# Two-layer transformer stack on one core: loads kept out of a recurrence, attention output and values by token block, gates spread without diagonals

## The reference

```
x = x + rwkv7(rms_norm(x))            # projections k, r, v, g and a small "lora"; recurrence in 4 chunks of 64 tokens
kb, vb = shared_kv(x)                 # k1, v1
x = x + moba(rms_norm(x), kb, vb)     # q1, gate g1; with 256 tokens: plain causal attention, 16 heads; then w_out
# second block, conditioned on a vector c:  ada = silu(c) @ ada_w + ada_b  gives shifts, scales and gates
h = modulate(rmsnorm(x)); y = mlstm(h)          # q2, k2, v2, input/forget gates, og, head norm, wo_c
x = x + gate * rmsnorm(y);  x = x + gate * rmsnorm(sqrelu_mlp(modulate(rmsnorm(x))))
h = modulate(rmsnorm(x)); y = mla(h, latent q and kv)   # cq, ckv, q_b, kv_b, 8 heads, wo_d
x = x + gate * rmsnorm(y);  x = x + gate * rmsnorm(sqrelu_mlp(modulate(rmsnorm(x))))
```

## Time and profile before

| | |
|---|---|
| median of three runs | 1046.74 us |
| the profiled execution, its device time | 1047.87 us |
| its span, first to last instruction | 1046.1 us |
| TensorE matmul busy | 993.2 us, 95% |
| VectorE busy | 752.1 us, 72% |
| ScalarE busy | 525.6 us, 50% |
| loads | 205.4 MB, mean 196 GB/s |

### The profile page before, as it was taken

One profiled execution on the slowest core, in us unless ns is written; L12 is line 12 of the kernel. 1 busy time (PEld: TensorE's weight loads), 2 busy tenths in 40 slices (PEclk: granted clock), 3 DMA queues, 4 the chain that ended last, 5 costly groups with the idle time before them and its releaser, 6 DMA issues.

```text
span 1046.1 us, 19356 instructions
## 1 busy us (share of the span) xinstructions
PE 993.2 (95%) x8274; PEld 864.8 (83%) x8274; DVE 752.1 (72%) x1277; ACT 525.6 (50%) x798; POOL 36.4 (3%) x33
## 2 busy tenths in 40 slices
PE   5999999968999999999999999999999899999996
PEld 4788899967788888788867899999688788999995
DVE  6789889577889958646589665676587895664544
ACT  3358431316454677455366445454466855445442
POOL 0000044200000100000000000000000000000000
PEclk9999999999999999999999999999999999999999
DMA  9674410492456550564264477776646444476411
GB/s 379 248 284 161 162 43 4 162 389 100 154 211 219 221 242 11 232 242 161 81 242 161 170 294 303 287 291 264 240 164 215 188 161 161 172 296 256 171 72 41
DMA packets 15222, 205.40 MB, mean 196 GB/s; under 512 B 1816, under 2 KB 1816, under 8 KB 2976
## 3 DMA queue, kind: packets, MB, share of 16 engines
q1 hardware_dynamic: 14544, 202.55, 50.5%
q10 hardware_dynamic: 592, 1.61, 0.5%
HBM read 203.10 MB, written 1.05 MB: 195 GB/s over the span
## 4 chain that ended last, share of the span: by engine, by line
PE 83%; DVE 10%; ACT 3%; issue 2%; DMA 1%; SPq 0%; DVEq 0%; ACTq 0%
PE bank L455 20%; PE bank L457 20%; PE bank L456 20%; PE bank L758 5%; PE bank L404 4%; DVE slot_parts L2019 2%; PE bank L661 1%; PE bank L562 1%; DMA ring<-in_stream 1%; PE bank L739 1%; PE bank L634 1%; DMA pc<-in_params 1%; PE bank L623 1%; PE bank L900 1%; PE bank L537 1%
## 5 line engine op out<-in xcount | busy, mean ns | idle before, releaser
L455 PE MATMUL bank<-page_parts 128*128 128x512 f32 (+3 forms) x1222 | 428.8, 351 | 6.8 <-DVE page_parts L2301 2.2
L2019 DVE TENSOR_TENSOR slot_parts<-ring,page_parts 128x2048 fp32r<-128x2048 f32 (+2 forms) x117 | 261.4, 2251 | 53.4 <-ACT page_parts L1356 52.9
L457 PE MATMUL bank<-page_parts 128*128 128x512 f32 (+2 forms) x750 | 291.4, 389 | 0.0
L456 PE MATMUL bank<-slot_parts,page_parts 128*128 128x512 f32 (+2 forms) x750 | 290.9, 388 | 0.0
L455 PEld LDWEIGHTS bank<-page_parts 128*128 128x128 f32 x1222 | 232.3, 190 | 36.5 <-issue 3.7
L1356 ACT ACTIVATE page_parts<-ring 128x2048 fp32r<-128x2048 f32 (+2 forms) x121 | 225.0, 1884 | 52.6 <-PE bank L457 28.1
L457 PEld LDWEIGHTS bank<-page_parts 128*128 128x128 f32 x750 | 141.3, 188 | 29.0
L456 PEld LDWEIGHTS bank<-slot_parts,page_parts 128*128 128x128 f32 x750 | 141.8, 189 | 26.8
L1434 ACT ACTIVATE arena<-bank 128x512 f32<-128x512 f32 (+2 forms) x134 | 74.2, 575 | 127.2 <-PE bank L457 67.0
L457 PE MATMUL bank<-page_parts,slot_parts 128*128 128x256 f32 x472 | 133.6, 283 | 0.0
L456 PE MATMUL bank<-page_parts 128*128 128x256 f32 x472 | 133.6, 283 | 0.0
(11 more groups left out here) (318 smaller groups left out, 1114.2 us busy)
## 6 DMA issues: line engine op xcount, KB each, us to landing
ring<-in_stream SPq DMA_DIRECT2D x95, 2048.0 KB, 8.0
arena<-in_x SPq DMA_DIRECT2D x2, 512.0 KB, 4.3
arena<-in_gn ACTq DMA_DIRECT2D x2, 512.0 KB, 4.4
out<-arena SPq DMA_DIRECT2D x2, 512.0 KB, 2.6
cc<-in_consts SPq DMA_DIRECT2D x1, 899.0 KB, 6.6
small<-in_cond ACTq DMA_DIRECT2D x1, 512.0 KB, 10.1
pc<-in_params SPq DMA_DIRECT2D x1, 287.0 KB, 6.8
arena<-in_head_sel ACTq DMA_DIRECT2D x1, 32.0 KB
```

The lines of the kernel that those rows point to most:

```text
L455: mm(out, a[0], b[0], start=start, stop=False)
L456: mm(out, a[0], b[1], start=False, stop=False)
L457: return mm(out, a[1], b[0], start=False, stop=stop)
L2019: tt(unit_parts(n)[1], lo, hi, ALU.subtract).then_inc(dv.step("w_lo"), 1)
```

## The change

- The TensorE program names two summed `ada` panels instead of six before the recurrence. With the order of the ring this puts `wo_a`'s two panels right behind them. SyncE's extra wait now stands at the first panel of `k1` and is for the state product of chunk 2. VectorE no longer sums quarters in the inversion's first levels and in the walk.
- The two direct panels at the end of the recurrence and ahead of the mLSTM are gone; they are summed. The panels taken out are summed elsewhere: three instead of two before the attention (12 quarters), one behind v2 and two behind k2 (4 and 8 quarters) instead of one, one in the head loop behind the fifth step of `og`, and eight instead of six in the first MLP.
- `wo_b` is made by `split_blocks`, with a fourth page; v2 by `split_blocks` is now the first product of the mLSTM stage, and q2 and k2 come behind the gates. The norm of each token block, its transposes and its scaling go beside the other block's products. In ScalarE's program the block's squares stand ahead of the split of the next v2 unit; in VectorE's program two quarters of that unit stand ahead of the block's norm.
- A gate is spread with the gate's column, broadcast along the free axis, as the stationary operand, and the identity as the moving one. The diagonals and the constant of ones are gone.
- In MLA VectorE splits two units of `kv_a` ahead of the query latent's norm and the third behind it.

```diff
-        ada_quarters = ({u: 2 for n in range(6) for u in (6 + 4 * n, 7 + 4 * n)}, {u: 2 for u in (10, 11, 14, 15)})
+        ada_before_down = ((1, 8), ())
+        ada_quarters = ({u: 2 for u in range(4, 30) if u % 4 > 1 or u in (4, 5, 28, 29)}, {u: 2 for u in (10, 11, 14, 15)})
...
             project_rows("g", G_PAGES, 1)
-            ada(6)
+            ada(2)
...
             rotation["at"] = 2
-            ada_direct()
             turn_block("yT", Yr, 0, lambda g: (sem("y_gated"), g + 1))
...
-                if (tb, n) == (0, 1):
-                    ada_turned()
-                elif (tb, n) == (1, 0):
+                if (tb, n) == (1, 0):
...
-            ada(2)
+            ada(3)
             pe.wait_ge(*evacuated(("q1T", 3)))
...
-            for half in range(2):
-                split_tok(("wo_b", half), split_parts(O1_PAGES), first_of(15, 16, 3), wait=("o1T_split", 0) if half == 0 else None)
+            def beside_wo_b(tb, n):
+                if (tb, n) == (1, 2):
+                    turn_block("hT_c", XN, 0, lambda g: (sem("xn"), 5))
+            def beside_v2(tb, n):
+                if (tb, n) == (0, 2):
+                    turn_block("hT_c", XN, 1, lambda g: (sem("xn"), 6))
+            split_blocks("wo_b", split_parts(O1_PAGES), from_first(15, 16, 3, 10), lambda tb, k: (sem("o1T_split"), k // 2 + 1), beside_wo_b)
             def spread(i):
+                pe.wait_ge(sem("gate_col"), i + 1)
...
-                        pe.wait_ge(sem("diag"), 8 * i + 4 * half + jj + 1)
-                        ins = mm(b[:, jj * P:(jj + 1) * P], ones, DIAG[:, 4 * half + jj, :], start=True, stop=True)
+                        ins = mm(b[:, jj * P:(jj + 1) * P], gcol[:, j:j + 1].to_broadcast([P, P]), ident, start=True, stop=True)
...
-            ada_direct()
-            pe.wait_ge(sem("xn"), 6)
-            transposes("hT_c", XN)
-            ada_turned()
             stage[0] = "mlstm"
-            for name in ("q2", "k2"):
-                split_T((name,), split_parts(MLSTM_PAGES), first_of(6, 14, 11), wait=("hT_c_split", 0) if name == "q2" else None)
-                if name == "q2":
-                    ada(1)
+            split_blocks("v2", split_parts(MLSTM_PAGES), from_first(6, 14, 1, 2), lambda tb, k: (sem("hT_c_split"), 2 * tb + k // 4 + 1),
+                         beside_v2)
...
             spread(0)
-            for half in range(2):
-                split_tok(("v2", half), split_parts(MLSTM_PAGES), first_of(6, 14, 11))
+            ada(1)
+            for name in ("q2", "k2"):
+                split_T((name,), split_parts(MLSTM_PAGES), from_first(11, 15, 16))
+            ada(2)
...
                     og_step(h - 1)
+                    if h == 5:
+                        ada(1)
...
-                if name == ("ada_rows", 5):
-                    sp.wait_ge(*finished(("X", 5, 3)))
+                if name == ("k1", 0):
+                    sp.wait_ge(*finished(("S", 2)))
...
             # ScalarE
+            for tb in range(TB):
+                x_block("wo_b", tb)
+                split(unit_of["v2", 0] + 2 + tb)
+                # scaling of hT_c, first four tiles of the block
...
             # VectorE
-            def gate_diagonal(i):
-                tt(gcol, ADA[:, at:at + 8], g, ALU.mult).then_inc(dv.step(), 1)
-                for j in range(KT):
-                    ts(DIAG[:, j, :], ident, gcol[:, j:j + 1], None, ALU.mult).then_inc(dv.step("diag"), 1)
+            def gate_column(i):
+                tt(gcol, ADA[:, at:at + 8], g, ALU.mult).then_inc(dv.step("gate_col"), 1)
...
+            u = unit_of["v2", 0]
+            split(u + 1)
+            for tb in range(TB):
+                add_to_x("wo_b", (tb,))
+                for q in range(2):
+                    split_quarter(u + 2 + tb, q)
+                norm_block(tb)
+                for q in range(2, 4):
+                    split_quarter(u + 2 + tb, q)
+                split_rows("hT_c", MLSTM_PAGES, 0, tb)
+            ada(4)
+            for _ in range(4):
+                next_unit(("q2", 0))
...
             gate_row(0)
+            ada(8)
             split(unit_of["og", 1] + 1)
...
-            split(unit_of["kv_a"] + 2)
+            split(unit_of["kv_a"] + 1)
             sq = head_sel
...
                 ins.then_inc(dv.step("cq_n" if tb else None), 1)
+            split(unit_of["kv_a"] + 2)
```

More of the change, by code:

```diff
@@ L77, in constants @@
     put("ident", np.eye(P))
-    put("ones", np.ones((P, P)))
     put("pair_ones", (p[:, None] // HD == p[None, :] // HD) * 1.0)
@@ L1806, in _ @@
             act(t_row[0:8, :], t_row[0:8, :], ACT.Ln, bias=1.0).then_inc(ac.step("gate_ln"), 1)
-            for half in range(2):
-                if half:
-                    act_.wait_ge(sem("m_total"), 1)
-                    act(em_row[0:8, :], mt_row[0:8, :], ACT.Exp, scale=-1.0).then_inc(ac.step("gate_rows"), 1)
-                    page_used.update({13: finished(("hT_c", 3)), 8: finished("gates")})
-                    split(unit_of["og", 1] + 1)
-                for tb in range(TB):
-                    copy(V2[:, tb, 4 * half:4 * half + 4, 0:DV], ("v2", half, tb))
+            for i in range(2):
+                split(ahead(("q2", i)))
+                pair([d[:, 2 * i:2 * i + 2, :] for d in Q2T_OF], ("q2", i))
+            act_.wait_ge(sem("m_total"), 1)
+            act(em_row[0:8, :], mt_row[0:8, :], ACT.Exp, scale=-1.0).then_inc(ac.step("gate_rows"), 1)
+            page_used.update({13: finished(("hT_c", 1, 1)), 8: finished("gates")})
+            copy(K2T[:, 0:2, :], ("k2", 0))
+            split(unit_of["og", 0] + 1)
+            copy(K2T[:, 2:4, :], ("k2", 1))
+            split(unit_of["og", 1] + 1)
             def h_squares(g):
@@ L2250, in _ @@
                                       ALU.subtract).then_inc(dv.frees((name, l, g)), 1)
-                    if l < 3 and g % 2:
-                        ada(1)
                 beside(l)
@@ L2440, in _ @@
             split_output("wo_b", "o1T", O1_PAGES)
-            split(unit_of["q2", 0] + 1)
-            add_to_x("wo_b")
             def modulation(first, last, modulated):
@@ L2659, in _ @@
                         finish_head(g - 1)
+                if 3 <= h < 7:
+                    ada(1)
                 if h == 7:
```

101 lines of the change are left out of this document (43 added, 58 removed).

## The result

The changed kernel takes 1080.2 us (median of four runs, 1077.8 to 1081.49), the kernel before 1046.65 beside it (1046.15 to 1050.27): a ratio of 1.031 with a 95% interval of 1.029 to 1.032. The forecast was 1056.3 with a range to 1063. The side was right; the loss is 33.5 us, not 9.6.

What follows compares the result with a forecast made beforehand. The prediction took TensorE, busy 95% of the span, as the bound. Its terms -13.3 + 3.5 + 6.5 + 11.2 + 2.8 - 2.2 + 1 = +9.5 gave 1057.4 us profiled, 1056.3 as median, range 1043 to 1063.

Steps and rivals of the forecast that it cites:

- Part 1: Inversion and chunk walk: without loads in the walk its issue breaks go, +2.0 in the inversion; sum -13.3 us.
- Part 2: Attention: wo_b's first panel comes late in the ring and ScalarE waits for it, +3.5 us (ends 2.5 and 4).
- Part 3: wo_b, norm and v2 by block: 5.9 us saved, 3.9 and 1.7 lost to late norms, 0.5 gained.
- Part 4: Head loop's start: the second og panel comes late; +6.5 us together with Part 3 (ends 3 and 9).
- Part 5: End of the head loop: wo_c's first panel comes one ring slot later, +11.2 us (ends 8 and 12).
- Part 6: First MLP: two more panels hide beside matmuls, but q_a comes late, +2.8 us (ends 1 and 4).
- Part 7: Diagonals and MLA's latent norm: TensorE's wait of 1.74 us goes, -2.1, and a smaller constant, -0.1.
- Clock: Half-rate stretches after the new breaks of about 4, 7 and 11 us: +1 us (0 to 5).
- `wo_c` does wait: Against the rival that the wo_c wait is hidden: Part 5 is 0, the time 1045.1 us; chance 0.13.
- all three late panels bite: Against the rival that none of Parts 2, 4 and 5's late panels bites: 1033.5 us; chance 0.10.
- the breaks of the walk are gone: Against the rival that the issue breaks stay: Part 1 about 0, the time 1069.6 us; chance 0.07.

Runs made afterwards that it cites:

- e13: e10 with SyncE's extra wait moved from the first k1 panel to the first wo_a panel, wo_a's first split behind it: 1043.4 us.
- e14: e10 without SyncE's extra wait, so the first k1 panel loads right behind wo_a's second: 1045.4 us.
- e3: The changed kernel with one number changed, where the PSUM bank rotation starts in the head loop: 1070.3 us.
- e2: The changed kernel with VectorE's order of quarters, og splits and gate-column copy changed ahead of and in the head loop: 1070.2 us.
- e1: The changed kernel with the ada panel at og's fifth step moved to the first MLP, its quarters at two more units: 1080.3 us.
- e5: As e1, but the ninth MLP panel is summed at two units behind the point where it is named: 1070.9 us.
- e10: e8 with eight instead of nine panels in the first MLP, the other named between the halves of v2: 1042.8 us, ratio 0.995.
- e8: The kernel before with the walk's change (panels summed elsewhere), the new gate spread and kv_a's third unit behind the latent norm: 1046.0 us, ratio 0.997.
- e4: The changed kernel with 44 and 48 idle matmuls in its two longest waits, head 0's scores and the last weighted product: 1079.1 us.
- e12: The changed kernel with late panels and quarters re-placed, e3's banks, and two ada panels ahead of wo_b instead of three: 1047.9 us, ratio 1.000.

## Why the prediction was wrong

- **Part 1** was right. The walk to `wo_a` -16.3 (forecast -15.3), the inversion +2.5 (+2.0). That loads cause the breaks is now shown by e13 and e14, not argued; their number is not quite one for each load.
- **Part 2** was right in place; the wait is 4.0 (3.5). The missed term is the clock: 6.8 us at half rate behind it, up to 2.4 us of loss, where I had one microsecond for all new breaks together.
- **Part 3** was right in its waits, 3.4 and 1.7 (3.9 and 1.7). Its own terms, 5.9 less 3.9 and 1.7, leave a gain of 0.3 and not 0.5.
- **Part 4 failed**, and with the clock it makes the prediction wrong: +18.2 in its stage where 7.0 stood (8.2 with the border of the rows put right). The false sentence is "TensorE's two `og` steps fill a part, and that is in both numbers": they don't, since head 0's scores want the bank of the gate columns, which VectorE frees last. From VectorE's last unit to the first weighted product it is 11.3 us instead of 2.5: the largest miss of one term, 8.8, of which some 2 are the half rate at which the first `og` step then runs. "The eight quarters put ahead of that split end before the panel is there and cost nothing" is nearly true in the chain as forecast: they end 1.6 us before the load, and push four units (8.9 us) and not two (4.5) behind them, but the panel was late anyway and VectorE ends only 0.9 us behind the forecast. (It never waits for the last units, as the prediction had expected.) With the bank free they do cost (4.8 us in e3). e3 prices the bank at 7.6 us of its stage and 10 of the median, e2 the order at 10.7; the two overlap, since e2 too has the columns copied early. Nothing in the trace of before showed the bank, since its count was another; it is in the code, where the order of the claims changed.
- **Part 5** was right in place and size: 11.5 (11.2), taken away in its stage by e1 and e5.
- **Part 6** was right where it looked (the pause at `q_a` is 3.1, forecast 2.8), but the stage lost 6.0 more than all its terms. e10 and e8 differ there by one panel's place, and by 4.7 us. TensorE idles 10.5 us in this stage instead of 7.2, a break of 2.3 at 566 us and one of 0.9 at 627 among them, both ended by VectorE's split of a unit; I had put the added panels at nothing for the reason that VectorE is a third idle there. Up to 3.7 us more are clock, up to 1.7 of them behind the pause.
- **Part 7**: the wait that it named is gone in the changed kernel and in e8; -1.2 in e8's stage, for -2.1.
- **Clock failed** as a term of the sum: +1 (0 to 5) on top of a gain of 3.5 in the walk, so -2.5 net. The time at half rate rose from 20 to 63 us, and the work done in it from 16.5 to 33.0 us, which makes TensorE's work 8.3 us longer. I had named the breaks and then given them one microsecond together. How much of the 8.3 reached the end of the kernel stays open: e4 takes away the two longest stretches, which by the same count cost 5.5 us, and its profiled execution is 3.4 shorter.

Each rival fell: `wo_c` does wait, all three late panels bite, and the breaks of the walk are gone. The range failed since its upper end was made of the bounds of terms that I had, part 4's "ends 3 and 9" held no case in which TensorE's own work can't fill the wait, and the clock's upper end was 5. By estimate, from 1080.2: without part 4's miss of some 10 us the time would still have been about 1070, outside the range; with the clock's other misses gone too (10.8, less the 2 counted in part 4) it would have been about 1061, inside it. The right side is no luck: the waits of parts 2, 3, 5 and 6 stand where they were forecast, each within a microsecond of its size.

## What to carry to other kernels

When work is put into the idle time of an engine that runs in order, the price is not only whether it ends before the late operand comes, but what ready work it pushes behind that operand, and above all who holds a buffer until then. Where the order of claims changes, list who gets which PSUM bank: a bank held by a small copy at the end of a long queue cost 10 us here, and one number took it away. Give each long wait a price for the clock behind it as well. A panel's place in a ring is a release time for the one four behind it: the 33 us lost by this change came back to a ratio of 1.000 (e12) by moving panels and quarters and by that one number, with the same work done.

## What the runs showed of the hardware

The issue breaks are TensorE's own instruction loads, late behind the data. In the counts of the load queues from 145 to 170 us (packets, MB, share of the engines), e14 (three panels loading) and e13 (none) differ so:

```profile
q8 instruction: 4, 0.07, 0.9%
```
```profile
q8 instruction: 6, 0.10, 1.8%
```

A packet of the instruction queue has 16 KB. In e14 they start at 153.03, 158.93 and 164.74 us, and a break of 1.9 us opens within 0.4 us of each, the first two ahead of 127 matmuls (with as many weight loads), which are one packet's worth. In e13, with the queues free, they come every 3.5 to 4.6 us, as fast as TensorE uses them up, and it never waits. Between 153.3 and 158.8 us e14's load engines are 99% busy with data and no instruction packet starts; in e13 two do. So the breaks go with packets rather than with loads: in the walk of the kernel before, six packets start while its seven loads run (203.3 to 235.3 us, 6.1 to 6.7 apart), and six breaks open, each within 1.6 us of one. Not every such packet brings a break: in e13's walk they start at 228.9, 235.7 and 240.2 us, and the third has none. A packet takes 0.9 to 1.5 us with or without loads beside it; what is late is its start. That it queues behind the data packets is the reading that fits, and no run separates it from another cause of a late start. The Trainium skill, "Runtime: NRT & Kernel Launch", section "Instruction fetch mechanics", says that blocks of 16 KiB with 256 instructions are fetched ahead and that crossing one is "mostly hidden". The block size agrees with the trace; the hiding holds for the long matmuls, in whose stages the kernel before has no such break under its loads, and not where 64x64 matmuls follow every 30 ns (760 in 23.00 us above) and a 2 MB load shares the engines. By its rule the walk would not have gained 16 us.
